# Strip sums of three feed-forward stages built in HBM by accumulating transfers, in the down tiles of the stage before

## The reference

```python
def half_swiglu(x, g, w_up, w_down):
    h = rms_norm(x, g)
    a, b = jnp.split(h @ w_up, 2, axis=-1)
    return x + 0.5 * ((jax.nn.silu(a) * b) @ w_down)

def layer(x, ...):
    x = half_swiglu(x, ffn1_norm, ffn1_up, ffn1_down)
    ...
    x = x + (g_a * y_a + g_b * y_b) @ w_out
    x = half_swiglu(x, ffn2_norm, ffn2_up, ffn2_down)
```

## Time and profile before

| | |
|---|---|
| time, median of 2 runs | 2734.81 us (2734.53 to 2735.08) |
| span of the profiled execution | 2732.7 us |
| outside the span, against the median | 2.1 us |
| TensorE busy | 2707.3 us, 99% of the span |
| VectorE, ScalarE, GpSimd busy | 1729.2, 1103.5, 999.8 us (63%, 40%, 37%) |
| mean granted TensorE clock | 0.998 of full |
| moved by DMA | 238.04 MB, 87 GB/s |

### The profile page before, as it was taken

The page is one execution under the profiler, slowest core; times in us unless marked ns, Lnnn a source line. Parts: engine busy times, 40 slices in busy tenths (PEclk is TensorE's granted clock), DMA queues, the critical chain, the costliest instruction groups (busy, mean ns, idle before and its releaser), DMA issues. The chain is left out here.

```text
span 2732.7 us, 46951 instructions
## 1 busy us (share of the span) xinstructions
PE 2707.3 (99%) x18804; PEld 2646.4 (97%) x18804; DVE 1729.2 (63%) x2801; ACT 1103.5 (40%) x1858; POOL 999.8 (37%) x610
## 2 busy tenths in 40 slices
PE   9999999999999999999999999999999999999998
PEld 8999999998999999999999999999989999999997
DVE  8747576887433693838685647668773347837475
ACT  5324244636322352424443333454463224424242
POOL 2333333345433333333333333333544333333332
PEclk9999999999999999999999999999999999999999
DMA  3222222233122222222222222222332222222222
GB/s 118 99 71 93 77 87 93 88 124 125 63 71 91 75 73 84 78 93 78 94 77 85 70 95 78 92 86 88 132 109 70 77 88 74 75 79 78 93 78 85
DMA packets 72853, 238.04 MB, mean 87 GB/s; under 512 B 8304, under 2 KB 17264, under 8 KB 72176
## 3 DMA queue, kind: packets, MB, share of 16 engines
q1 hardware_dynamic: 57888, 208.30, 22.1%
q10 hardware_dynamic: 14800, 27.51, 2.9%
HBM read 227.52 MB, written 8.27 MB: 86 GB/s over the span
## 5 line engine op out<-in xcount | busy, mean ns | idle before, releaser
L498 POOL TENSOR_TENSOR w_lo<-w_raw,w_hi 128x1024 fp32r<-128x1024 f32 (+1 forms) x254 | 600.0, 2365 | 962.8 <-ACT w_hi L1131 947.7
L1131 ACT ACTIVATE w_hi<-w_raw 128x1024 fp32r<-128x1024 f32 (+1 forms) x238 | 250.2, 1051 | 796.1 <-PE lin L635 660.8
L635 PE MATMUL lin<-h_hi,w_hi 128*128 128x320 f32 x1600 | 373.8, 315 | 2.9 <-DVE tmp L1614 2.7
L635 PE MATMUL lin<-h_hi,w_lo 128*128 128x320 f32 x1600 | 364.6, 309 | 0.0
L635 PE MATMUL lin<-h_lo,w_hi 128*128 128x320 f32 x1600 | 364.1, 309 | 0.0
L635 PE MATMUL lin<-g_hi,w_lo 128*128 128x320 f32 x1408 | 320.9, 309 | 0.0
L635 PE MATMUL lin<-g_lo,w_hi 128*128 128x320 f32 x1408 | 320.8, 309 | 0.0
L635 PE MATMUL lin<-g_hi,w_hi 128*128 128x320 f32 x1408 | 320.7, 309 | 0.0
L550 POOL TENSOR_TENSOR lo_A<-raw_even,hi_A 128x512 fp32r<-128x512 f32 x120 | 167.8, 1398 | 376.3 <-ACT hi_A L1185 376.3
L635 PEld LDWEIGHTS lin<-h_hi,w_hi 128*128 128x128 f32 x1600 | 265.2, 188 | 15.9 <-issue 11.3
L635 PEld LDWEIGHTS lin<-h_lo,w_hi 128*128 128x128 f32 x1600 | 267.5, 188 | 0.0
(11 more groups left out here) (334 smaller groups left out, 6215.6 us busy)
## 6 DMA issues: line engine op xcount, KB each, us to landing
w_raw<-wts SPq DMA_DIRECT2D x240, 512.0 KB, 3.5
raw_even<-wts SPq DMA_DIRECT2D x88, 512.0 KB, 4.4
raw_odd<-wts SPq DMA_DIRECT2D x64, 512.0 KB, 4.2
caches<-kcache_in ACTq DMA_DIRECT2D x16, 512.0 KB, 4.0
caches<-vcache_in ACTq DMA_DIRECT2D x16, 512.0 KB, 4.7
x<-x_in SPq DMA_DIRECT2D x8, 320.0 KB, 6.6
k_out<-kT ACTq DMA_DIRECT2D x2, 1280.0 KB, 4.6
v_out<-v_sb ACTq DMA_DIRECT2D x2, 1280.0 KB, 8.6
```

Source lines behind the costliest of these rows:

```text
L498: ins = nc.gpsimd.tensor_tensor(w_lo[:, s, cols], w_raw[:, s, cols], w_hi[:, s, cols].bitcast(F), ALU.subtract)
L635: ins = nc.tensor.matmul(out[:, half, :], w, a[:, half * HALF:(half + 1) * HALF], start=first and n == 0, stop=last and n == 2)
L1131: nc.scalar.activation(w_hi[:, s, 0:cols], w_raw[:, s, 0:cols], ACT.Copy).then_inc(hi_ready.sem, 1)
```

## The change

A tensor `made` in HBM holds the four sums for each of the 19 pairs of the stages (0, 1), (1, 0) and (1, 1). They are built while the stage before runs its down tiles, two **slots** for each tile, 48 in a stage. SyncE copies one strip of the weights to the place of each sum (`open_sums`, four transfers of 256 KB for a pair, in the two slots of one tile). GpSimd then adds the other operand with a transfer that accumulates (`add_sums`). S1 and S3 take a strip of the weights. S2 takes S1 as it is in HBM, and S4 takes S2. Before each, GpSimd waits until the place is opened, until the last sum of that name has landed, and for S2 and S4 until the sum that is their operand has landed. In tile k of a stage GpSimd issues after `low`: S2 of pair k-1, S4 of pair k-2, S1 of pair k, S3 of pair k.

In the three stages served this way (`from_dram`) VectorE's `add_strips` returns at once. SyncE loads the pair with three transfers (a tile of 512 KB, the ready S3, and strip 3) and the sums S1, S2 and S4 with one each (`load_sum`, 256 KB), behind waits of their own; ScalarE's `hi_strip` waits for those landings. Since an accumulating transfer here adds only, the signs are arranged so that all four sums of strips are additions; the sums of tokens (T1 to T4) and the steps that combine products (u2, u3, c21, c22) swap additions and subtractions for it, in the same number and shape. The first stage, (0, 0), keeps its sums on VectorE, with the new signs.

```diff
+        made = nc.dram_tensor("strip_sums", (2 * DEPTH - 1, NP, 4, P, 4 * P), F, kind="Internal").ap()
+        SUMS = ("S1", "S2", "S3", "S4")
...
+        pair_in = [ctx.enter_context(nc.semaphore(f"pair_in_{k}")) for k in ("even", "odd")]
+        S1_in = ctx.enter_context(nc.semaphore("S1_in"))
+        S2_in = [ctx.enter_context(nc.semaphore(f"S2_in_{k}")) for k in ("even", "odd")]
+        S4_in = [ctx.enter_context(nc.semaphore(f"S4_in_{k}")) for k in ("even", "odd")]
+        sum_opened = {k: ctx.enter_context(nc.semaphore(f"opened_{k}")) for k in SUMS}
+        sum_added = {k: ctx.enter_context(nc.semaphore(f"added_{k}")) for k in SUMS}
...
-                sp.wait_ge(sums_done["S4"].sem, sums_done["S4"].count(L, q + 1))
+                if from_dram(L, q):
+                    sp.wait_ge(strip_ready["A11"].sem, strip_ready["A11"].count(L, q + 1))
+                    sp.wait_ge(strip_ready["A12"].sem, strip_ready["A12"].count(L, q + 1))
+                else:
+                    sp.wait_ge(sums_done["S4"].sem, sums_done["S4"].count(L, q + 1))
                 sp.wait_ge(strip_ready["A22"].sem, strip_ready["A22"].count(L, q + 1))
...
+                if from_dram(L, q):
+                    sp.wait_ge(sum_added["S3"], 16 * ((2 * L - 1) * NP + q + 1))
+                    sp.dma_start(raw_[:, 0:2, :].rearrange("p a n -> p (a n)"), wts[n]).then_inc(sem, 16)
+                    sp.dma_start(raw_[:, 2, :], made[2 * L + q // NP - 1, q % NP, 2]).then_inc(sem, 16)
+                    sp.dma_start(raw_[:, 3, :], wts[n + 1][:, 4 * P:]).then_inc(sem, 16)
+                else:
+                    for j in range(2):
+                        sp.dma_start(raw_[:, 2 * j:2 * j + 2, :].rearrange("p a n -> p (a n)"), wts[n + j]).then_inc(sem, 16)
...
+                if name == "S1":
+                    sp.wait_ge(strip_ready["S1"].sem, strip_ready["S1"].count(L, q))
+                    to = S1_sum
+                elif name == "S2":
+                    sp.wait_ge(strip_ready["S4"].sem, strip_ready["S4"].count(L, q if i == 0 else q - 1))
+                    to = S2_sum[i % 2]
+                elif early:
+                    sp.wait_ge(product_done["M3"].sem, product_done["M3"].count(L, q))
+                    to = S4_sum
+                else:
+                    sp.wait_ge(strip_ready["S2"].sem, strip_ready["S2"].count(L, q + 1))
+                    to = S2_sum[i % 2]
+                sp.wait_ge(sum_added[name], 16 * ((2 * L - 1) * NP + q + 1))
+                sem, _ = sum_landed(L, q, name)
+                sp.dma_start(to[:, :], made[2 * L + q // NP - 1, q % NP, SUMS.index(name)]).then_inc(sem, 16)
...
+            def load_first(L, q):
+
+                load_pair(L, q, 0, q // NP * (FFN_WEIGHTS + MIX_TILES) + 2 * PLAIN)
+                load_sum(L, q, 0, "S1")
+                load_sum(L, q, 0, "S2")
+                load_sum(L, q, 0, "S4", early=True)
+
+            def open_sums(L, f, slot):
+
+                k, second = divmod(slot, 2)
+                fi = 2 * L + f + 1
+                if k >= NP or fi >= 2 * DEPTH:
+                    return
+                n = pair_weight(fi, k)
+                for name, src in (("S2", wts[n][:, 0:4 * P]), ("S4", wts[n][:, 4 * P:])) if second else (
+                        ("S1", wts[n + 1][:, 0:4 * P]), ("S3", wts[n][:, 0:4 * P])):
+                    sp.wait_ge(sum_opened[name], 16 * ((fi - 1) * NP + k))
+                    sp.dma_start(made[fi - 1, k, SUMS.index(name)], src).then_inc(sum_opened[name], 16)
...
+                slots = iter(range(BUILD_SLOTS))
                 for g, pairs in enumerate(SEGMENTS):
-                    for i in range(pairs):
+                    for i in range(pairs + 2):
                         if i == 1:
                             sp.wait_ge(lo_ready.sem, lo_ready.count(L, n))
-                        if i:
+                            if g == 0 and from_dram(L, q):
+                                sp.wait_ge(evacuated.sem, evacuated.count(L, (0, FFN2_RES)[f] + 2 * PLAIN))
+                        if 2 <= i and (g or i > 2):
+                            load_sum(L, q + i - 2, i - 2, "S4")
+                        if 2 <= i <= pairs:
+                            load_sum(L, q + i - 1, i - 1, "S1")
+                        if 1 <= i < pairs:
                             load_pair(L, q + i, i, w + 2 * i)
+                            load_sum(L, q + i, i, "S2")
                     w += 2 * pairs
                     for j in range(KB):
                         if j < 2:
                             load(L, n + j, w + j, after_odd=q + (pairs - 1) // 2 * 2 - 1)
                         else:
                             load(L, n + j, w + j)
+                        open_sums(L, f, next(slots))
+                        open_sums(L, f, next(slots))
                         if j == 3 and g < len(SEGMENTS) - 1:
                             pair_free(L, q + pairs - 1)
                             load_pair(L, q + pairs, 0, w + KB)
-                        if j == 1 and g == len(SEGMENTS) - 1 and f and L < DEPTH - 1:
+                            load_sum(L, q + pairs, 0, "S1")
+                            load_sum(L, q + pairs, 0, "S2")
+                        if j == 3 and g == len(SEGMENTS) - 1 and f and L < DEPTH - 1:
                             pair_free(L, q + pairs - 1)
-                            load_pair(L + 1, 0, 0, 2 * PLAIN)
+                            load_first(L + 1, 0)
                     n, w, q = n + KB, w + KB, q + pairs

             for L in range(DEPTH):
@@ -478,7 +574,8 @@
                     load(L, MIX_AT + n, FFN_WEIGHTS + n)
                     if n == MIX_TILES - KB + 1:
                         sp.wait_ge(o_kept.sem, o_kept.count(L, NI))
-                        load_pair(L, NP, 0, FFN_WEIGHTS + MIX_TILES + 2 * PLAIN)
+                        sp.wait_ge(evacuated.sem, evacuated.count(L, GATE_RES + 1))
...
+            def add_sums(L, f, slot):
+
+                fi = 2 * L + f + 1
+                if fi >= 2 * DEPTH:
+                    return
+                for name, at_, other in (("S1", 1, None), ("S3", 1, None), ("S2", 2, "S1"), ("S4", 4, "S2")):
+                    k, rest = divmod(slot - at_, 2)
+                    if rest or not 0 <= k < NP:
+                        continue
+                    n, done = pair_weight(fi, k), (fi - 1) * NP + k
+                    pool.wait_ge(sum_opened[name], 16 * (done + 1))
+                    pool.wait_ge(sum_added[name], 16 * done)
+                    if other:
+                        pool.wait_ge(sum_added[other], 16 * (done + 1))
+                        src = made[fi - 1, k, SUMS.index(other)]
+                    else:
+                        src = wts[n + 1][:, 4 * P:] if name == "S1" else wts[n + 1][:, 0:4 * P]
+                    nc.gpsimd.dma_start(made[fi - 1, k, SUMS.index(name)], src,
+                                        accum_op=ALU.add, max_dma_last_dim=4096).then_inc(sum_added[name], 16)
...
@@ -568,6 +686,8 @@
                             low_strip(L, q + i + 1, i + 1, "A12")
                     for k in range(KB):
                         low(L, n + k)
+                        add_sums(L, f, next(slots))
+                        add_sums(L, f, next(slots))
...
                 if name[0] == "A":
-                    sem, count = pairs_landed(L, q)
+                    sem, count = raw_count(L, q)
+                    act.wait_ge(sem, count)
+                elif from_dram(L, q):
+                    sem, count = sum_landed(L, q, name)
                     act.wait_ge(sem, count)
                 else:
                     act.wait_ge(sums_done[name].sem, sums_done[name].count(L, q + 1))
...
             def add_strips(L, q, i, name):

+                if from_dram(L, q):
+                    return
...
-                    out, a, b, op = S2_sum[i % 2][:, :], S1_sum[:, :], raw_[:, 0, :], ALU.subtract
+                    out, a, b, op = S2_sum[i % 2][:, :], S1_sum[:, :], raw_[:, 0, :], ALU.add
...
-                    out, a, b, op = raw_[:, 2, :], raw_[:, 0, :], raw_[:, 2, :], ALU.subtract
+                    out, a, b, op = raw_[:, 2, :], raw_[:, 0, :], raw_[:, 2, :], ALU.add
...
-                nc.vector.tensor_tensor(u2[i % 2], middle[i % 2], u1[i % 2], ALU.add).then_inc(u2_kept.sem, 1)
+                nc.vector.tensor_tensor(u2[i % 2], u1[i % 2], middle[i % 2], ALU.subtract).then_inc(u2_kept.sem, 1)
```

More of the change, by code:

```diff
@@ L407, in pairs_landed, with raw_count, from_dram, sum_landed @@
             per_ffn = sum((n + 1 - side) // 2 for n in SEGMENTS)
-            before = sum((n + 1 - side) // 2 for n in SEGMENTS[:g])
-            return pair_in[side].sem, pair_in[side].count(L, 32 * (f * per_ffn + before + i // 2 + 1))
+            nth = sum((n + 1 - side) // 2 for n in SEGMENTS[:g]) + i // 2 + 1
+            back = per_ffn * (2 * L + f - 1)
+            return side, nth, back, per_ffn
+        def raw_count(L, q):
```

(40 more changed lines are left out.)

17 lines of the change are left out of this document (9 added, 8 removed).

## The result

The changed kernel takes 2857.0 us (2855.3 to 2858.7, 2 runs) against 2734.81 us: ratio 1.0448, interval 1.0431 to 1.0465. The forecast was 2848 us. Four further runs on another chip gave 2855.7 us, ratio 1.0444 (1.0427 to 1.0462).

A forecast was written before the change was run, and what follows sets the result against it. TensorE bounds the kernel, busy 2707.3 of 2732.7 us. Late `low` adds 14.6 and 23.1 us, 37.7 us a stage, 113 us in three stages: 2845.7 us of span, with 2.1 us outside it 2848 us; range 2748 to 3000 us.

The forecast's parts named there:

- Nothing from VectorE, pairs or signs: Whole kernel: 226 us less VectorE work, the swapped signs and larger pair loads were each put at nothing.
- The price of an accumulation: Down tiles: an accumulating 256 KB transfer takes two streams, 1.52 us, bounded by 0.76 and 2.28 us.
- The rival in which HBM on both sides costs twice: Down tiles: each read and write counts, turn 16.7 us, 3068 us in all, or 2956 us halfway; chance 0.20.
- The turn: Down tiles: one round of GpSimd's loop of `low` and four issues, taken as 10.6 us, the tile's DMA time.
- The floor of the chain without queues: Down tiles: three issues, one transfer and a landing on GpSimd take 3 + 1.5 + 1.5 = 6 us.
- GpSimd holds `low`, TensorE waits: Down tiles: in-order GpSimd waits for S1 to land, delaying the next `low`; TensorE waits 3 to 4 us a tile.
- Segment 1: Down tiles of segment 1: `low` of tile 7 comes late by 23.1 us a stage, in three stages.
- the formula: Segment 1: lateness of `low` of tile 7 is six GpSimd turns less 40.5 us, nothing below a 6.7 us turn.
- Segment 0: Down tiles of segment 0: six GpSimd turns less 49.0 us, 14.6 us late a stage, in three stages.
- two corrections are of opposite sign, and I let them cancel: First two tiles of segment 0 lack S2 and S4; next pair's loads add 4.6 us in tile 3; net nothing.
- Segment 2: Down tiles of segment 2: pairs run out after full tiles 0 to 2, backlog gone before tile 7, loss nothing.
- The form of the loss: TensorE gaps of 3 to 4 us a tile in tiles 4 to 7 of segments 0 and 1, dense in segment 2.

The follow-up runs named there:

- the run without building: Changed kernel without the HBM copies and accumulating transfers; the served stages load weight strips in place of sums: 2735.92 us, ratio 1.0005.
- plain copies: Changed kernel with GpSimd's transfers copying instead of adding, same count, order and waits, and without the limit `max_dma_last_dim`: 2761.59 us, ratio 1.0096.
- two in flight: Changed kernel with two counters for each sum name and S2 and S4 issued two and four slots later: 2839.53 us, ratio 1.0391.
- three sums: Changed kernel without the accumulation of S4, whose place keeps the copied strip: 2795.98 us, ratio 1.0225.
- busy GpSimd: Kernel before the change, plus nine small GpSimd operations behind each `low` of segments 0 and 1, no transfer added: 2856.45 us, ratio 1.0443.
- the filled gaps: Changed kernel plus 16 unused matmuls ahead of each of tiles 4 to 7 of segments 0 and 1: 2869.19 us, again 2869.96 us.

## Why the prediction was right, and where it wasn't

- **Nothing from VectorE, pairs or signs: right.** Shown by the run without building (ratio 1.0005).
- **The price of an accumulation: right.** 1.52 us taken, 1.49 measured (all 228 of them: 11.7% of 2856.8 us, 1.47 each). That two reads are the reason was argued, and no run shows it. The lower bound, one stream, was what plain copies cost, 0.73 us. The rival in which HBM on both sides costs twice falls with that number. 262144 bytes in 0.73 us are 359 GB/s. The prediction also leant on 207 to 214 GB/s for copies between HBM tensors (the Trainium skill, "DMA: Bandwidth & Descriptors", "Latency and other measured facts"). The page gives these for rows of 16 KiB laid out hundreds of KiB or more apart, and they don't carry over to the rows of 2 KB here.
- **The turn: right.** 10.6 us forecast, 10.2 to 10.6 measured in full tiles, at a DMA share of 1.0. That it is the engines' time and not the wait as such is shown by two in flight (chain cut, turn of segment 1 still 10.1 to 10.5) and by plain copies and three sums (less DMA time, shorter turn). The floor of the chain without queues, 6 us, left out S2 and S4, two transfers of 1.5 us by its own price. It didn't decide here.
- **GpSimd holds `low`, TensorE waits: right.** Its place, its 79.6 us, and the dense stage (1, 1) are as forecast; busy GpSimd shows that this link is enough by itself.
- **Segment 1: right in sum.** 69.3 us forecast for three stages, 70.3 measured. At the measured turns the formula gives 22.7 us a segment, and it lost 23.4. Two small things cancel in it: `low` of the last tile was 21.5 us late in the first of them (342.97 against 309.07 + 12.43), and behind it came the slow tile, 3 us longer.
- **Segment 0: too high,** 43.8 against 34.3 us. The step that failed is "two corrections are of opposite sign, and I let them cancel". The light first tiles weighed more than the next pair's loads. GpSimd, `low` of the tiles 1, 2, 3 and 7 in the first stage, after:

```profile
120.95 3.02 POOL L595 TENSOR_TENSOR w_lo<-w_raw,w_hi 128x1024 fp32r<-128x1024 f32 x1
...
132.06 2.41 POOL L595 TENSOR_TENSOR w_lo<-w_raw,w_hi 128x1024 fp32r<-128x1024 f32 x1 [2.64 <-ACT w_hi L1251]
...
139.01 2.41 POOL L595 TENSOR_TENSOR w_lo<-w_raw,w_hi 128x1024 fp32r<-128x1024 f32 x1
...
179.91 3.57 POOL L595 TENSOR_TENSOR w_lo<-w_raw,w_hi 128x1024 fp32r<-128x1024 f32 x1
```

  The two turns ahead of tile 3 take 18.1 us and not 21.2, and for the first of them GpSimd waits at its end for ScalarE, as before the change. The other four take 40.9 us, 42.4 by forecast. `low` of tile 7 ends at 183.48, forecast 187.3.
- **Segment 2: wrong,** 0 against 16.5 us. The step that failed is "the backlog is gone before tile 7: nothing". Tiles 0 to 2 are full, so `low` of tile 3 (457.54 + 2.67) makes TensorE wait 3.35 us, and the tile then takes 8.0 us. The backlog of GpSimd does run out after that, but a loss of an engine that is 99% busy isn't made good. A lateness has to be looked at in each tile, and the largest counts, not the last.
- **The form of the loss: partly unforeseen.** I expected gaps; a third of it shows as slower matmuls. By the filled gaps that is mostly another face of the same waiting.

So that 2848 lies as near to 2857 us as it does is in part luck: two errors of opposite sign, 9.5 us too much in segment 0 and 16.5 us too little in segment 2. The mechanism and the largest term stand.

## What to carry to other kernels

Before work is moved off an engine, look whether the engine that sets the end ever waits for it; here 226 us of VectorE were worth nothing, and a cover of 76% idle DMA engines was the only thing spent. Price a transfer that adds as two plain ones of its size (the ratio measured here), sum the engines' time for each tile of the critical engine, and see what an engine that waits for landings holds back behind itself. If such transfers are wanted, spread them over the whole stage: the same 228 cost 122 us in the down tiles and at most 8 us spread.

## What the runs showed of the hardware

- Accumulating transfers from HBM to HBM, as issued here, took 1.47 to 1.67 us of the 16 engines for 256 KB, plain ones 0.73; a plain HBM-to-HBM copy was as cheap as a load.
- GpSimd issued four accumulating transfers in 3.1 us, 0.8 us each (I had taken 1). In other turns `low` begins 2.1 to 2.8 us after the first issue and is longer by as much, so that both end 5.7 to 5.8 us after it all the same. Plain copies took it 0.5 us each.
- TensorE's clock didn't go by the length of the last gap alone. In the first stage, behind gaps of 3.4, 4.4 and 4.8 us, the matmuls began at the lower level and stayed there for 5 to 6 us. Behind gaps of 3.35 and 4.0 us they began at the full one, fell after about 1 us, and were back 3.2 to 3.6 us later. Behind a gap of 3.0 us nothing happened. In the next stage one of 2.27 us (at 1280.75, behind two tiles that had run partly at the lower level) was enough to begin low.
- More transfers in flight didn't raise what was moved (273 GB/s, against 255 to 276 in the changed kernel's windows): at a share of 1.05 the wait went from one queue's landings to the other's.
